# Dilated attention heads: probability scaling in halves of two blocks, one slot apart

## The reference, cut to what matters

```python
def dilated_mixer(qkv):
    for g, (w, d) in enumerate(DIL_GROUPS):        # ((128, 1), (512, 4), (2048, 16))
        o, lse = dilated_window_group(q, k, v, w, d)
    ...
    wts = jax.nn.softmax(jnp.stack(lses, 0), axis=0)
    o = jnp.sum(wts[..., None] * jnp.stack(outs, 0).astype(F32), axis=0)
```

## Time and profile before

| | us |
|---|---|
| median of 3 runs | 2047.54 (2047.39 to 2049.02) |
| the profiled execution | 2052.49 |
| its span in the profile | 2050.7 |
| PE busy in it | 2007.5 (98%) |
| DVE busy | 1080.8 (53%) |
| ACT busy | 805.3 (39%) |
| POOL busy | 418.0 (20%) |

### The profile page before, as it was taken

One profiled execution on the slowest core, in us unless ns is written; L12 is line 12 of the kernel. 1 busy time (PEld: TensorE's weight loads), 2 busy tenths in 40 slices (PEclk: granted clock), 3 DMA queues, 4 the chain that ended last, 5 costly groups with the idle time before them and its releaser, 6 DMA issues. The chain is left out here.

```text
span 2050.7 us, 27177 instructions
## 1 busy us (share of the span) xinstructions
PE 2007.5 (98%) x9869; PEld 1639.2 (80%) x9869; DVE 1080.8 (53%) x1940; ACT 805.3 (39%) x1463; POOL 418.0 (20%) x343
## 2 busy tenths in 40 slices
PE   7999999999999999999999999999999999999998
PEld 4688888888888787888888788788888888767787
DVE  7734444445645645645635432697878783334312
ACT  5433323343433433433534411544444443223322
POOL 3232413323323323323310011401010100000011
PEclk9999999999999999999999999999999999999999
DMA  7331331533233232332335420411111111512422
GB/s 248 118 134 64 122 124 41 149 93 90 67 102 94 63 103 67 88 103 77 78 131 173 149 62 21 140 37 36 44 39 43 39 43 47 153 52 99 148 62 103
DMA packets 218352, 186.98 MB, mean 91 GB/s; under 512 B 9498, under 2 KB 191236, under 8 KB 217604
## 3 DMA queue, kind: packets, MB, share of 16 engines
q1 hardware_dynamic: 212960, 177.56, 28.6%
q0 software_dynamic: 4480, 6.66, 1.3%
q10 hardware_dynamic: 804, 1.33, 0.2%
HBM read 144.27 MB, written 41.25 MB: 90 GB/s over the span
## 5 line engine op out<-in xcount | busy, mean ns | idle before, releaser
L300 DVE TENSOR_TENSOR w_lo<-w_raw,w_hi 128x512 fp32r<-128x512 f32 x219 | 190.8, 872 | 166.2 <-ACT w_hi L296 166.0
L220 PE MATMUL z_ps<-b_parts,w_hi 128*128 128x512 f32 x680 | 274.8, 404 | 2.3 <-ACT g_gate L230 1.8
L222 PE MATMUL z_ps<-b_parts,w_lo 128*128 128x512 f32 x680 | 268.3, 395 | 0.0
L221 PE MATMUL z_ps<-b_parts,w_hi 128*128 128x512 f32 x680 | 268.1, 394 | 0.0
L323 PE MATMUL z_ps<-ah_hi,w_hi 128*128 128x512 f32 x512 | 210.7, 412 | 7.9 <-DVE w_lo L300 2.6
L325 PE MATMUL z_ps<-ah_hi,w_lo 128*128 128x512 f32 x512 | 202.7, 396 | 0.0
L324 PE MATMUL z_ps<-ah_lo,w_hi 128*128 128x512 f32 x512 | 202.5, 396 | 0.0
L296 ACT ACTIVATE w_hi<-w_raw 128x512 fp32r<-128x512 f32 x224 | 138.3, 624 | 104.8 <-PE z_ps L325 54.0
L220 PEld LDWEIGHTS z_ps<-b_parts,w_hi 128*128 128x128 f32 x680 | 128.1, 188 | 35.1 <-issue 7.2
L222 PEld LDWEIGHTS z_ps<-b_parts,w_lo 128*128 128x128 f32 x680 | 128.0, 188 | 30.1
L221 PEld LDWEIGHTS z_ps<-b_parts,w_hi 128*128 128x128 f32 x680 | 128.2, 189 | 28.2 <-issue 0.5
(11 more groups left out here) (500 smaller groups left out, 4366.5 us busy)
## 6 DMA issues: line engine op xcount, KB each, us to landing
w_raw<-in_a_win SPq DMA_DIRECT2D x160, 256.0 KB, 3.1
w_raw<-in_b_win SPq DMA_DIRECT2D x33, 512.0 KB, 4.0
work<-in_a_win SPq DMA_DIRECT2D x48, 256.0 KB, 5.2
v_scratch<-qkv SPq DMA_DIRECT2D x12, 1024.0 KB, 5.2
work<-v_scratch SPq DMA_DIRECT2D x16, 512.0 KB, 5.3
y_scratch<-y SPq DMA_DIRECT2D x16, 512.0 KB, 3.4
w_raw<-in_a_wout SPq DMA_DIRECT2D x8, 768.0 KB, 5.6
w_raw<-in_b_wout SPq DMA_DIRECT2D x8, 768.0 KB, 6.3
```

The lines of the kernel that those rows point to most:

```text
L220: pe.matmul(z_ps[s][:, 0:width], w_hi[slot][:, k, :], hi[k][:, tok], start=(k == 0), stop=False)
L221: pe.matmul(z_ps[s][:, 0:width], w_hi[slot][:, k, :], lo[k][:, tok], start=False, stop=False)
L222: mm = pe.matmul(z_ps[s][:, 0:width], w_lo[slot][:, k, :], hi[k][:, tok], start=False, stop=(k == nk - 1))
L300: eng.tensor_tensor(op_ring(w_lo, u), op_raw[i], op_ring(w_hi, u).bitcast(F32), ALU.subtract).then_inc(lo_op, 1)
```

## The change

The four blocks of a group are multiplied in two halves, one slot apart, and each half raises `p_ready`. The turn of a half waits for its half alone. The first half of the residue blocks stays behind `join` in slots 27 and 31, the second goes to 28 and 32. The first half of the natural blocks stays in 30 and 34, the second goes to 31 and 35. In slot 31 the natural half of `s = 1` stands ahead of `join` of `s = 0`. The number of multiplications and their shapes don't change.

```diff
-                        pe.wait_ge(p_ready, 4 * h + which + 1)
+                        pe.wait_ge(p_ready, NT * h + n + 1)
...
                         dve.wait_ge(fac_done, n + 1)
-                        for r in range(RES):
+
+                    def scale_residues(s, half):
+                        for r in range(2 * half, 2 * half + 2):
                             out = dve.tensor_scalar(x[s][:, TPS + r, :], x[s][:, TPS + r, :], fac[s][:, 1, r:r + 1], None,
                                                     ALU.mult)
                         out.then_inc(p_ready, 1)
 
-                    def scale_natural(h, s):
+                    def scale_natural(h, s, half):
                         dve.wait_ge(fac_in, 16 * ordinal(h, s) + 16)
-                        for t in range(TPS):
+                        for t in range(2 * half, 2 * half + 2):
                             out = dve.tensor_scalar(x[s][:, t, :], x[s][:, t, :], fac_nat[s][:, t:t + 1], None, ALU.mult)
                         out.then_inc(p_ready, 1)
...
                     def attention(h, u):
+                        if u in (30, 31, 34, 35):
+                            scale_natural(h, 1 if u < 32 else 0, u % 2)
                         if u in (27, 31):
                             join(h, 1 if u == 27 else 0)
-                        if u in (30, 34):
-                            scale_natural(h, 1 if u == 30 else 0)
+                        if u in (27, 28, 31, 32):
+                            scale_residues(1 if u < 30 else 0, 0 if u in (27, 31) else 1)
```

## The result

| | before | after |
|---|---|---|
| median, us | 2048.28 (2047.39 to 2054.23, 4 runs) | 2072.94 (2069.94 to 2092.99, 4 runs) |
| ratio | | 1.0137 (95%: 1.0108 to 1.0166) |
| profiled execution, us | 2052.49 | 2069.94 |
| its span, us | 2050.7 | 2068.2 |

The kernel is slower by 1.4%. That is the side and, as the traces show, the main mechanism of the forecast. The time lies 4.5 us above the forecast of 2068.4 and 1.4 us above the upper end of its range. The profiled execution is the fastest of its four, 3.0 us under their median.

A forecast was written before the change was run, and what follows sets the result against it. PE, busy for 98% of the span, was taken to bound the kernel. Slot 32's 2.38 us per head plus slot 31's shifts less slack made 20.8 us: span 2050.7 to 2071.5, median 2068.4; range 2047.0 to 2071.5.

The forecast's parts named there:

- The path to the eviction: DVE and POOL steps from T to the eviction of product 4: forecast start T + 6.77, before T + 4.39.
- T: Start of the first residue multiplication behind the second join; forecast 0.48 us later in heads 0, 2, 5, 6, 7.
- The choice on which it hung: Slot 32: whether the last residue multiplication slips in before POOL's line 1210 or stands behind lines 1210 and 1215.
- the late value: Slot 32: last multiplication stands behind lines 1210 and 1215, so the eviction comes 2.38 us later in each head.
- Rival A: Slot 32: the last multiplication gets in ahead of line 1210; only slot 31's 1.7 us remain, 2049.3 us; chance 0.30.
- B: Slot 32: some heads slip through and some are held; half of them, some 11 us, 2059 us; chance 0.08.
- Rival C: Slot 32: the transfer of line 1210 alone blocks; eviction at T + 4.84, 5.3 us, 2052.9 us; chance 0.06.
- Rival D: Low part at T + 1.13 gets in ahead of line 283; eviction 1.08 us sooner, 2044.6 us; chance 0.04.
- The natural pair ahead of the join: Slot 31: pair waits for line 279, join 0.48 us later in heads 0, 2, 5, 6, 7; 1.7 us after slack.
- The sum: Waits on PE's path before slot 34's product: 2.38 us per head plus slot 31's shifts less slack, together 20.8 us.
- From the profiled execution to the median: Whole kernel: profiled execution taken as 4.95 us above the median, so 2073.3 us became 2068.4.

The follow-up runs named there:

- group 3: Experiments on what holds the fourth multiplication, against the changed kernel: slopes_late, load_late, and one with the held pair as a single two-input instruction (2048.78 us).
- slopes_late: Changed kernel with POOL's slope addition (line 1215) moved behind two later weight sums; 2063.53 us, ratio 1.0088; run again 2060.69 us, ratio 1.0044.
- load_late: Changed kernel with the load of the factors (line 1210) issued behind the slope addition (line 1215) instead of ahead; 2066.80 us, ratio 1.0099.
- after_again: The changed kernel run once more, unaltered; 2079.42 us, ratio 1.0152.
- res_only: Changed kernel with only the residue blocks in halves, the natural blocks whole in slots 30 and 34 as before; 2076.67 us, ratio 1.0145.
- nat_only: Changed kernel with only the natural blocks in halves, the residue blocks all four behind the join as before; 2049.09 us, ratio 1.0012.
- behind_evict: Changed kernel with the second residue pair of the first sequence moved from slot 32 to slot 33, behind the eviction of product 4; 2050.53 us, ratio 1.0010.

## Why the prediction was right or wrong

**The path to the eviction: right, to 0.02 us.** Forecast and measured, from T: low part ends 2.89 and 2.90 (554.37 + 1.78), line 287 ends 4.04 and 4.05, fourth multiplication starts 4.12 and 4.12, line 1210 starts 3.99 and 4.00, line 1215 ends 6.69 and 6.70, the eviction starts 6.77 and 6.78. It holds in all eight heads.

**The choice on which it hung: right, with a reason that needed mending.** The forecast took the late value since nine of ten multiplications that had started just behind a transfer stood behind the tensor operation after it. Rival A (it slips through) had 0.12 us as enough; at 0.12 to 0.13 us it slipped through in no head. B (mixed) falls with it. The choice was close, though: group 3 has the turning point near 0.1 us, and the one that slipped through at 0.12 us stays unexplained. The mended reason is that of group 3: with no tensor operation queued behind the transfer, the multiplication runs beside it (*slopes_late*); with the operation ahead of the transfer, it is held all the same (*load_late*).

**Rival C: refuted.** The transfer alone would have let the multiplication in when line 1210 ended, with the eviction at T + 4.84. It came at T + 6.78, and in *slopes_late* the multiplication ran while the transfer was under way. The Trainium skill (SBUF — State Buffer, "SBUF: two separate sides") has the first to start hold the port "for the whole instruction"; the traces here agree where one tensor operation stands directly behind another (the low part that starts 0.09 us after line 283 waits for its end), and not around a transfer that GpSimd issues: it neither holds the multiplication for its 0.77 us, nor does its end let it in, and the multiplication that starts 0.67 us ahead of line 1215 does not go first.

**Rival D: refuted.** The low part at 0.09 us behind line 283 stood behind it, in all heads.

**The natural pair ahead of the join: the shift is there, the heads are not quite the same.** DVE and POOL in head 0 answer to the earlier trace rows:

```profile
470.68 1.64 DVE L1514 TENSOR_SCALAR work<-work,fac_nat 128x256 f32<-128x256 f32 x2
472.25 0.15 DVE L1489 TENSOR_TENSOR top<-both 128x4 f32<-128x4 f32 x1
...
470.34 1.57 POOL L279 TENSOR_TENSOR w_raw<-w_raw 128x512 f32<-128x512 f32 x1
```

The join starts 0.34 us after line 279 ends (471.91), as forecast. It does so in six heads (0 and 3 to 7) where five were named; head 2 was among the five, but there the sums came late and the join stood idle for them. In the account of the kernel after the moves of T come to 21.5 - 8 x 2.39 = 2.4 us, where 1.7 were forecast. The nearness is in part luck. By head the added losses are 2.6, 2.7, 3.7, 2.1, 1.8, 3.0, 2.7 and 2.9 us, so that head 2 (forecast 2.9) and head 4 (2.4) miss in opposite ways. T also moves against PE without the natural pair: in *res_only* the same account leaves 22.8 - 19.1 = 3.7 us, in *nat_only* 5.1. What moves it there is open.

**The sum: 21.5 us of waits, forecast 20.8; the step that failed took each wait to cost its length alone.** The term that was missing is TensorE's clock, 4.3 us in the profiled execution. The forecast gave the product behind each wait its undisturbed 3.24 us; two of eight took 5.96 and 4.82, and in *after_again* more did. The kernel before has waits of at most 1.1 us in front of this product and not one stretch of the lower level in the heads, so its trace had nothing to read the term from. It did have a stretch of 3.4 us at 73.8 us into the span, and eight new waits of 2.4 us and more should have been given an upper bound by it. The range ended at 2071.5, which is the forecast with 0.26 us more per head and a little spread, as if a wait could cost only its own length; it had to allow for some 2 us behind each of the longer waits, and for the kernel's stops at the loop's edges, of which the profile before showed one (2.6 us).

**From the profiled execution to the median: a second weak step.** The forecast took off 4.95 us, by which the profiled execution of the kernel before lay above its median, and so took the profiled execution of the kernel after to lie as far above its own. For the profiled execution itself it said 2073.3 us, and 2069.94 were measured: 3.4 us less, not more. The median of the kernel after lies 3.0 us above its profiled execution. The 24.7 us between the medians fit the 21.5 of waits and some 3 to 4 of lower level, but the executions that make up the median have no trace, so this split is argued and not shown.

## What to carry to other kernels

Splitting work so that its first half can be used sooner pays only if somebody waits for the first half; here nobody did, and the second half got a place of its own in a queue for what VectorE and GpSimd share. Before a VectorE instruction is moved, look what GpSimd has queued at its new place: behind the transfers that GpSimd issues here, it is the next tensor operation that counts, even if that starts later. And a wait of some microseconds on a TensorE that is otherwise always busy can cost its length and more (2.7 us more behind the 3.7 us of head 2), so the upper end of a range has to hold that too.

## What the hardware showed that I had not expected

- A 128x256 multiplication that starts 0.12 to 0.13 us after GpSimd's issue of a transfer (line 1210) is held until 0.16 us after the tensor operation behind it, up to 2.74 us; without such an operation it takes 0.34 us beside the same transfer. In *behind_evict* this holds also for one that starts 0.52 us after the transfer's start. The turning point lies near 0.1 us: six of six at 0.01 to 0.09 us after line 1201 got through, while at 0.09 to 0.10 us after line 1206 none did.
- The steps from T to the eviction come at the same distances in all heads, to within 0.03 us, so such a queue can be forecast step by step.
- TensorE at its lower level behind waits of 2.3 to 4.0 us, for 3.4 or 6.8 us, not each time: matmuls of 128x512 every 0.43 us, not every 0.23.
- Stops of all engines for 2.2 to 4.0 us at two edges of a loop, in step with packets in an instruction queue, in 14 of 26 cases. Two of them and what follows them cost 12.3 us in *slopes_late*; the times of one kernel spread over 10 to 15 us.
